# Order of the large and small matmuls in the column slots of a TensorE-bound block stack

## Chip, core and metric

The kernel runs on one core of one Trainium2 chip. The metric is the device time of one execution in microseconds (us); the kernel before takes 1665.5 us, the median of three runs.

## What is computed

Three transformer-like blocks over 256 tokens of width 1024, in float32: two layers of a first block and one of a second. Each has two gated feed-forward parts (FFN, inner width 2816) around a mixer. What matters here is the FFN and the second mixer, named sc:

```python
def swiglu(h, w_gate, w_up, w_down):
    return (jax.nn.silu(h @ w_gate) * (h @ w_up)) @ w_down
...
            p = h @ c_w_in[o]                       # 1024 -> 3 * 1024
            gate_b = p[..., :SC_WIDTH]
            gate_c = p[..., SC_WIDTH:2 * SC_WIDTH]
            xt = p[..., 2 * SC_WIDTH:]
            mix = (gate_b * causal_depthwise_conv(gate_c * xt, c_conv_w[o])) @ c_w_out[o]
```

## The kernel before

TensorE works on numbers split in two: a rounded high part in the type fp32r, and the low rest. A product of x and w is built as w_hi*x_hi + w_hi*x_lo + w_lo*x_hi, all added up in a PSUM bank.

The weights come from HBM as 564 slots of 128 x 1024 numbers into a ring `raw` of four. For each slot ACT writes the rounded part `w_hi` (line 1135), DVE the rest `w_lo` (line 1764 or 1768), both into a ring of eight, and PE uses it; the semaphore `lo_ready` tells PE that a slot is there, `slot_used` gives it back. SP issues the loads of `raw` in order (line 410). The order of work on each engine is written out by hand.

The eleven sub-stages run one after the other: ffn_0, ab, ffn_1, ctx_ffn, ffn_2, ctx_mix, sc, ffn_3, ffn_4, ssd, ffn_5. An FFN has eleven steps of 256 inner columns. In ffn_0 and in the first two and the last step of every FFN, gate and up products are made with tokens as the stationary operand (`wide_slot`, line 494). In the steps j = 2 to 9 of the other six FFN passes, and in all 24 input slots of sc, the weights are stationary: `column_slot` (lines 515 to 529). One such slot has the weights of 128 output columns for all eight k-tiles of the width of 1024 and fills one PSUM bank of 512 numbers for each partition. For each k-tile it issues two matmuls:

- a large one, with the 128 x 128 piece of `w_hi` stationary and 512 moving columns, the 256 tokens of the high part of hT and the 256 of its low part (`hT[:, :, k, :]`, two pieces of 256);
- a small one, with the piece of `w_lo` stationary and the 256 tokens of the high part alone, added onto the first half of the bank.

Each matmul has a weight load of its own. Even k-tiles issue large, small (lines 524 and 525) and odd ones small, large (lines 527 and 528), so that in a slot the order is L S S L L S S L and so on, and the last matmul, a large one, signals `slot_used`. The two halves of the bank are added up afterwards by ACT and DVE.

An FFN step with column slots (line 679 on) runs four of them, two for the gate in the banks `gu` and two for the up product in the banks `tp`, then the two down slots of the step before (`down`, line 539), each with 12 large matmuls whose moving operand is one piece of 512. A few transposes stand in between in the first steps. In sc, 24 column slots follow each other with other work between some. `col_slot` (line 509) is another helper, with small matmuls alone, used by other stages.

Of the kernel before, what the change touches and what calls it, by code (L numbers as in the profile page):

```python
# [23 lines left out]
KT = D // P  # L24
TOK = 256
TT = TOK // P
# [111 lines left out]
def build(nc, weights, ada_w, x_in, ctx_in, pre_rows, post_rows, small, mod, out):  # L138
    with ExitStack() as stack:
        def sb(name, shape, dt=F32):  # L140
            return stack.enter_context(nc.sbuf_tensor(name, shape, dt))

        def sem(name):
            return stack.enter_context(nc.semaphore(name))

        raw = sb("raw", [P, RAW, SLOT])
        w_hi = sb("w_hi", [P, RING, SLOT], F32R)
        w_lo = sb("w_lo", [P, RING, SLOT], F32R)
        hT = sb("hT", [P, 2, KT, TOK], F32R)
        hT_hi, hT_lo = hT[:, 0, :, :], hT[:, 1, :, :]  # L150
# [130 lines left out]
        hT_psum, hT_hi_ready, hT_lo_ready = sem("hT_psum"), sem("hT_hi_ready"), sem("hT_lo_ready")  # L281
# [47 lines left out]
        def any_bank(b):  # L329
            return dn_bank(b) if b < 4 else gu[:, b - 4, :] if b < 6 else tp[:, b - 6, :]  # L330
# [24 lines left out]
        def sc_bank(q):  # L355
            return any_bank(SC_BANKS[q])
# [32 lines left out]
        def column_bank(si):  # L389

            return (gu, tp)[si // 2][:, si % 2, :]
# [60 lines left out]
        def _(pe):  # L452
# [27 lines left out]
            def wide_slot(n, si, banks, used=True, between=lambda: None):  # L480

                if n < 2:
                    pe.wait_ge(lo_half, n + 1)
                else:
                    pe.wait_ge(lo_ready, n + 1)
                r = n % RING
                for kk in range(2):
                    if n < 2 and kk:
                        between()
                        pe.wait_ge(lo_ready, n + 1)  # L490
                    k = 2 * si + kk
                    for t, bank in banks.items():
                        for q, (h, w) in enumerate(((hT_hi, w_hi), (hT_lo, w_hi), (hT_hi, w_lo))):
                            m = pe.matmul(bank, h[:, k, t * P:(t + 1) * P],  # L494
                                          w[:, r, kk * 512:(kk + 1) * 512],
                                          start=k == 0 and q == 0, stop=k == KT - 1 and q == 2)
                if used:
                    m.then_inc(slot_used, 1)
                return m
# [12 lines left out]
                        m.then_inc(half_done, 1)  # L512
                m.then_inc(slot_used, 1)

            def column_slot(n, o, at_half=lambda: None):

                pe.wait_ge(lo_ready, n + 1)
                r = n % RING
                for k in range(KT):
                    if k == KT // 2:  # L520
                        at_half()
                    c = slice(k * P, (k + 1) * P)
                    if k % 2 == 0:
                        pe.matmul(o, w_hi[:, r, c], hT[:, :, k, :], start=k == 0, stop=False)  # L524
                        pe.matmul(o[:, 0:TOK], w_lo[:, r, c], hT_hi[:, k, :], start=False, stop=False)  # L525
                    else:
                        pe.matmul(o[:, 0:TOK], w_lo[:, r, c], hT_hi[:, k, :], start=False, stop=False)  # L527
                        m = pe.matmul(o, w_hi[:, r, c], hT[:, :, k, :], start=False, stop=k == KT - 1)  # L528
                m.then_inc(slot_used, 1)

            def down_slot(n, acts, k, start=False, stop=False, used=True):
# [95 lines left out]
            def ffn(s, n0):  # L627
# [3 lines left out]
                def act_transposed(j):  # L631
                    pe.wait_ge(act_ready, GATE_N[s, j, 1])
                    for t in range(TT):
                        for kk in range(2):
                            m = pe.transpose(tp[:, 0, kk * TOK + t * P:kk * TOK + (t + 1) * P],
                                             act_tok[:, t, kk * P:(kk + 1) * P], ident[:])
                    m.then_inc(actT_psum, 1)
# [8 lines left out]
                def down(n, j):  # L646
                    pe.wait_ge(actT_lo_ready, TURN_N[s, j, 1 if s and j == 0 else None])
                    for kk in range(2):
                        down_slot(n + kk, tokens_of(actT_hi, actT_lo, range(TT)), kk, start=j == 0 and kk == 0)
# [6 lines left out]
                def mod_transposed(group):  # L656
                    pe.wait_ge(ada_used, ADA_GROUP * (group + 1))
                    cols = mod_cols[:, ADA_GROUP * group:ADA_GROUP * (group + 1), :].rearrange("p i v -> p (i v)")
                    pe.transpose(tp[0:2 * ADA_GROUP, 1, 0:P], cols, ident[:]).then_inc(mod_turned, 1)
# [18 lines left out]
                for j in range(2, STEPS - 1):  # L678
                    n = n0 + 10 + 6 * (j - 2)
                    if s == 0:  # L680
                        if j > 2:
                            act_transposed(j - 1)
                        for si in range(4):
                            wide_slot(n + si, si, both)
                        down(n + 4, j - 1)
                        continue
                    for si in range(4):
                        if j > 2 and si % 2 == 0:
                            pe.wait_ge((gate_summed, up_summed)[si // 2], COLUMN_N[s, j - 1])
                        elif si == 2:  # L690
                            pe.wait_ge(actT_lo_ready, TURN_N[s, 1, None])
                        if si == 3 and (s, j - 1) in ADA_TURN:
                            pe.wait_ge(mod_biased, 1 + ADA_TURN[s, j - 1])
                        column_slot(n + si, column_bank(si))
                    down(n + 4, j - 1)
                    if (s, j) in ADA_TURN:
                        pe.wait_ge(up_summed, COLUMN_N[s, j])
                        mod_transposed(ADA_TURN[s, j])
# [23 lines left out]
                else:  # L722
                    for t in range(TT):
                        for si in range(4):
                            m = wide_slot(end + si, si, {t: gu[:, t, :]}, used=t == 1)
# [132 lines left out]
            def sc(s, n0):  # L858
                for q in range(3 * KT):
                    if q == 1:  # L860
                        context_x_tokens(1)
                    if q == 4:
                        context_b_tokens()
                    if q == 7:
                        context_states()
                    if q == 8:
                        pe.wait_ge(state_ready, 2)
                    if SC_BEFORE[q] is not None:
                        pe.wait_ge(sc_summed, SC_BEFORE[q] + 1)
                    if q:  # L870
                        column_slot(n0 + q, sc_bank(q))
                    else:
                        pe.wait_ge(hT_lo_ready, 2 * TT * s + TT)
                        column_slot(n0, sc_bank(0), lambda: pe.wait_ge(hT_lo_ready, 2 * TT * (s + 1)))
                out_proj(s, n0 + 3 * KT, range(KT), [[MIX0["sc"] + 1 + k // 2] * TT for k in range(KT)], apart=(0, 1))

            def dt_slot(n):
# [50 lines left out]
            def context_x_tokens(t):  # L928
                pe.wait_ge(conv_done, 4 + t)
                pe.wait_ge(xbc_ready, 3)  # L930
                for i in range(SSD_W // P):
                    m = turned_tile(x_cols[:, t * SSD_W + i * P:t * SSD_W + (i + 1) * P], 0, XS_T + i, t)
                if t:
                    m.then_inc(tokT_psum, 1)

            def context_b_tokens():
                pe.wait_ge(xbc_ready, 5)
                pe.wait_ge(p_ready, 1)
                for t, bank in enumerate((x_cols[:, TT * SSD_W:], x_cols[:, 0:512])):
                    if t:  # L940
                        pe.wait_ge(tok_ready, TT)
                    for i in range(SSD_G):
                        m = turned_tile(bank[:, i * P:(i + 1) * P], 0, BM_T + i, t)
                m.then_inc(tokT_psum, 1)

            def context_states():
                pe.wait_ge(tok_ready, 2 * TT)
                pe.wait_ge(xdt_ready, 2)
                for d in range(2):
                    for g in range(SSD_G):  # L950
                        for t in range(TT):
                            m = pe.matmul(dn[:, d, g * 256:g * 256 + GW], bm_tok[:, t, g * P:(g + 1) * P],
                                          x_dt_ctx[d][:, t, g * GW:(g + 1) * GW], start=t == 0, stop=t == 1)
                    m.then_inc(state_psum, 1)
# [173 lines left out]
            for s, name in enumerate(SUB):  # L1128
                {"ctx_mix": ctx_mix, "ab": ab, "sc": sc, "ssd": ssd}.get(name, ffn)(s, BASE[name])
# [1584 lines left out]
```

## Time and profile before

| what | value |
|---|---|
| median of three runs | 1665.5 us (1664.55 to 1665.92) |
| profiled execution | 1664.43 us |
| its span, first to last instruction | 1662.6 us |
| granted TensorE clock, mean | 0.999 |
| PE busy | 1654.5 us |
| PE weight loads busy | 1414.6 us |
| DVE busy | 1228.0 us |
| ACT busy | 928.0 us |
| large matmuls of column slots | 1728 |
| small matmuls of column slots | 1728 |

Matmuls are pipelined: a record's length reaches beyond the start of the next one, so what one costs on PE is the distance between starts. In the chain of waits a row covers these distances, not lengths. A timeline row shows the start and the length; rows of the same form that overlap can be merged, with their count.

### The profile page before, as it was taken

Reading aid. Unit: us, or ns where it says so; the run is one execution under the profiler, and the core shown is the slowest. Engines: PE = TensorE matmul, PEld = TensorE weight load, DVE = VectorE, ACT = ScalarE, POOL = GpSimd, SP = SyncE. Lnnn points to the kernel's source line nnn. Section 1 sums busy time; section 2 is a strip of 40 time slices with the busy share of each in tenths; the row PEclk is TensorE's granted clock in tenths of the full one; section 3 lists DMA queues with packets and bytes.
Section 4 is the critical chain, followed back from the end, with each engine's and each line's share of the span. In section 5 each row is a group of like instructions: output and inputs, shape, how many; then the busy total and the mean of one; then the engine's idle time right before and its main releaser. Section 6 shows DMA issues by size and latency. Waiting matters only on the chain.

```text
span 1662.6 us, 22804 instructions
## 1 busy us (share of the span) xinstructions
PE 1654.5 (100%) x8756; PEld 1414.6 (85%) x8756; DVE 1228.0 (74%) x1630; ACT 928.0 (56%) x1396; POOL 152.1 (9%) x210
## 2 busy tenths in 40 slices
PE   9999999999999999999999999999999999999998
PEld 7888888888888888888899888888888889988887
DVE  6888776788889777776688876655766568986564
ACT  6555577645555555555566455554645458655553
POOL 1100100000211001020010011000012011311000
PEclk9999999999999999999999999999999999999999
DMA  8977553787859776787655558654667546357551
GB/s 297 332 266 258 172 190 103 245 295 259 287 172 331 267 247 215 255 302 256 205 166 185 169 173 266 201 191 139 226 215 251 187 144 202 110 180 243 189 190 64
DMA packets 99356, 359.32 MB, mean 216 GB/s; under 512 B 11184, under 2 KB 11440, under 8 KB 99248
## 3 DMA queue, kind: packets, MB, share of 16 engines
q1 hardware_dynamic: 92736, 335.59, 59.6%
q0 software_dynamic: 6368, 22.21, 4.5%
q8 instruction: 69, 1.13, 0.3%
q14 instruction: 39, 0.32, 0.1%
q10 hardware_dynamic: 144, 0.07, 0.0%
HBM read 356.70 MB, written 1.12 MB: 215 GB/s over the span
## 4 chain that ended last, share of the span: by engine, by line
PE 98%; DVE 1%; DMA 0%; issue 0%; SPq 0%; ACT 0%; DVEq 0%; POOLq 0%; POOL 0%; ACTq 0%
PE dn L539 29%; PE gu L494 21%; PE gu L528 6%; PE tp L528 6%; PE gu L524 6%; PE tp L524 6%; PE dn L509 5%; PE gu L527 3%; PE tp L527 3%; PE gu L525 3%; PE tp L525 3%; PE tp L457 1%; PE gu L509 1%; PE dn L494 1%; PE dn L528 0%; PE dn L524 0%
## 5 line engine op out<-in xcount | busy, mean ns | idle before, releaser
L1768 DVE TENSOR_TENSOR w_lo<-raw,w_hi 128x1024 fp32r<-128x1024 f32 x520 | 639.5, 1240 | 216.3 <-ACT w_hi L1135 211.2
L1135 ACT ACTIVATE w_hi<-raw 128x1024 fp32r<-128x1024 f32 x520 | 549.5, 1059 | 319.5 <-PE dn L539 145.4
L494 PE MATMUL gu<-w_hi,hT 128*128 128x512 f32 x1056 | 328.9, 393 | 0.9 <-DVE w_lo L1764 0.5
L539 PE MATMUL dn<-w_hi,actT_hi 128*128 128x512 f32 x608 | 238.8, 393 | 0.0
L539 PE MATMUL dn<-w_lo,actT_hi 128*128 128x512 f32 x608 | 236.9, 390 | 0.0
L539 PE MATMUL dn<-w_hi,actT_lo 128*128 128x512 f32 x608 | 236.8, 389 | 0.0
L494 PEld LDWEIGHTS gu<-w_hi,hT 128*128 128x128 f32 x1056 | 195.6, 188 | 42.5 <-DVE hT L1776 1.4
L494 PE MATMUL gu<-w_lo,hT 128*128 128x512 f32 x528 | 205.8, 390 | 0.0
L524 PE MATMUL gu<-hT,w_hi 128*128 128x512 f32 x416 | 165.2, 397 | 0.0
L528 PE MATMUL gu<-hT,w_hi 128*128 128x512 f32 x416 | 164.6, 396 | 0.0
L524 PE MATMUL tp<-hT,w_hi 128*128 128x512 f32 x416 | 164.5, 396 | 0.0
L528 PE MATMUL tp<-hT,w_hi 128*128 128x512 f32 x416 | 164.5, 396 | 0.0
L1912 DVE CUSTOM_DVE_ANT_0 arena<-arena 128x1024 f32<-128x1024 f32 x112 | 135.0, 1231 | 0.3
L539 PEld LDWEIGHTS dn<-w_lo,actT_hi 128*128 128x128 f32 x608 | 114.1, 188 | 24.1
L539 PEld LDWEIGHTS dn<-w_hi,actT_lo 128*128 128x128 f32 x608 | 114.2, 188 | 23.4
L539 PEld LDWEIGHTS dn<-w_hi,actT_hi 128*128 128x128 f32 x608 | 114.2, 188 | 21.2
L494 PEld LDWEIGHTS gu<-w_lo,hT 128*128 128x128 f32 x528 | 99.1, 188 | 21.0
L527 PE MATMUL gu<-hT,w_lo 128*128 128x256 f32 x416 | 115.8, 278 | 0.0
L527 PE MATMUL tp<-hT,w_lo 128*128 128x256 f32 x416 | 115.8, 278 | 0.0
L525 PE MATMUL gu<-hT,w_lo 128*128 128x256 f32 x416 | 115.4, 277 | 0.0
L525 PE MATMUL tp<-hT,w_lo 128*128 128x256 f32 x416 | 115.4, 277 | 0.0
L2467 POOL TENSOR_SCALAR ms<-ssq 128x1 f32<-128x1 f32 x42 | 17.8, 425 | 926.4 <-ACT junk L1166 912.8
(366 smaller groups left out, 2506.2 us busy)
## 6 DMA issues: line engine op xcount, KB each, us to landing
raw<-in_weights SPq DMA_DIRECT2D x563, 512.0 KB, 4.3
arena<-in_ada_w SPq DMA_DIRECT2D x72, 512.0 KB, 4.4
post_row<-in_post_rows POOLq DMA_DIRECT2D x10, 512.0 KB, 6.2
pre_row<-in_pre_rows POOLq DMA_DIRECT2D x10, 512.0 KB, 7.4
mod_row<-mod POOLq DMA_DIRECT2D x9, 512.0 KB, 9.8
shift_row<-mod POOLq DMA_DIRECT2D x5, 512.0 KB, 10.0
x<-in_x_in SPq DMA_DIRECT2D x4, 256.0 KB, 5.7
arena<-in_c_rows POOLq DMA_DIRECT2D x2, 512.0 KB, 8.8
```

Source lines behind the costliest of these rows:

```text
L457: m = pe.transpose(in_bank(s, t, half)[:, q * P:(q + 1) * P], rows[:, t, k * P:(k + 1) * P], ident[:])
L494: m = pe.matmul(bank, h[:, k, t * P:(t + 1) * P], w[:, r, kk * 512:(kk + 1) * 512], start=k == 0 and q == 0, stop=k == KT - 1 and q == 2)
L509: m = pe.matmul(o, w[:, r, k * P:(k + 1) * P], h[:, k, :], start=k == 0 and q == 0, stop=k == KT - 1 and q == 2)
L524: pe.matmul(o, w_hi[:, r, c], hT[:, :, k, :], start=k == 0, stop=False)
L525: pe.matmul(o[:, 0:TOK], w_lo[:, r, c], hT_hi[:, k, :], start=False, stop=False)
L527: pe.matmul(o[:, 0:TOK], w_lo[:, r, c], hT_hi[:, k, :], start=False, stop=False)
L528: m = pe.matmul(o, w_hi[:, r, c], hT[:, :, k, :], start=False, stop=k == KT - 1)
L539: m = pe.matmul(dn[:, t, c], a[:, k, :], w[:, r, c], start=start and q == 0, stop=stop and q == 2)
L1135: act.activation(o, i, ACT.Copy, **kw).then_inc(done, 1)
L1768: dve.tensor_tensor(w_lo[:, r, :], raw[:, n % RAW, :], w_hi[:, r, :].bitcast(F32), ALU.subtract).then_inc(lo_ready, 1)
L1912: m = dve.tensor_tensor_reduce(ada_out[:, v, :], w, c_row[:, v, :], 1.0, 0.0, ALU.mult, ALU.add, mod_cols[:, i, v:v + 1])
L2467: pool.tensor_scalar(ms[:, c], ssq[:, c, 0], eps, None, ALU.add).then_inc(pool_step, 1)
```

## The change

`column_slot` gets a flag `lead`. Without it every k-tile issues large, small. With it k-tile 1 alone issues small, large, so that the slot begins L S S L and goes on L S L S. The flag is set in the first of the four slots of an FFN step and in the first slot of sc. The last matmul of a slot is now always a small one, and that one signals `slot_used`.

```diff
-            def column_slot(n, o, at_half=lambda: None):
+            def column_slot(n, o, at_half=lambda: None, lead=False):
 
                 pe.wait_ge(lo_ready, n + 1)
                 r = n % RING
@@ -520,12 +520,12 @@
                     if k == KT // 2:
                         at_half()
                     c = slice(k * P, (k + 1) * P)
-                    if k % 2 == 0:
+                    if lead and k == 1:
+                        pe.matmul(o[:, 0:TOK], w_lo[:, r, c], hT_hi[:, k, :], start=False, stop=False)
+                        pe.matmul(o, w_hi[:, r, c], hT[:, :, k, :], start=False, stop=False)
+                    else:
                         pe.matmul(o, w_hi[:, r, c], hT[:, :, k, :], start=k == 0, stop=False)
-                        pe.matmul(o[:, 0:TOK], w_lo[:, r, c], hT_hi[:, k, :], start=False, stop=False)
-                    else:
-                        pe.matmul(o[:, 0:TOK], w_lo[:, r, c], hT_hi[:, k, :], start=False, stop=False)
-                        m = pe.matmul(o, w_hi[:, r, c], hT[:, :, k, :], start=False, stop=k == KT - 1)
+                        m = pe.matmul(o[:, 0:TOK], w_lo[:, r, c], hT_hi[:, k, :], start=False, stop=k == KT - 1)
                 m.then_inc(slot_used, 1)
...
-                        column_slot(n + si, column_bank(si))
+                        column_slot(n + si, column_bank(si), lead=si == 0)
...
-                        column_slot(n0, sc_bank(0), lambda: pe.wait_ge(hT_lo_ready, 2 * TT * (s + 1)))
+                        column_slot(n0, sc_bank(0), lambda: pe.wait_ge(hT_lo_ready, 2 * TT * (s + 1)), lead=True)
```

## Rows read from the trace of the kernel before

**Rows 1.** The page: busy time of the engines, granted clock by slice, chain by engine.
```profile
PE 1654.5 (100%) x8756; PEld 1414.6 (85%) x8756; DVE 1228.0 (74%) x1630; ACT 928.0 (56%) x1396; POOL 152.1 (9%) x210
...
PEclk9999999999999999999999999999999999999999
...
PE 98%; DVE 1%; DMA 0%; issue 0%; SPq 0%; ACT 0%; DVEq 0%; POOLq 0%; POOL 0%; ACTq 0%
```

**Rows 2.** Waits of PE: us in total, times, longest us.
```profile
PE dn L594 <- DVE actT_hi L2441: 1.5, 1, 1.5
PE gu L494 <- DVE w_lo L1764: 0.5, 1, 0.5
PE gu L494 <- DVE w_lo L1768: 0.3, 1, 0.3
```

**Rows 3.** Timeline of PE, a step's column slots: start us, length us, line, tiles.
```profile
558.48 0.39 PE L539 MATMUL dn<-w_lo,actT_hi 128*128 128x512 f32 x1
558.71 0.39 PE L524 MATMUL gu<-hT,w_hi 128*128 128x512 f32 x1
...
559.16 0.40 PE L528 MATMUL gu<-hT,w_hi 128*128 128x512 f32 x1
559.40 0.40 PE L524 MATMUL gu<-hT,w_hi 128*128 128x512 f32 x1
...
561.49 0.39 PE L524 MATMUL gu<-hT,w_hi 128*128 128x512 f32 x1
561.72 0.28 PE L525 MATMUL gu<-hT,w_lo 128*128 128x256 f32 x1
561.83 0.28 PE L527 MATMUL gu<-hT,w_lo 128*128 128x256 f32 x1
561.95 0.40 PE L528 MATMUL gu<-hT,w_hi 128*128 128x512 f32 x1
562.18 0.40 PE L524 MATMUL gu<-hT,w_hi 128*128 128x512 f32 x1
562.42 0.28 PE L525 MATMUL gu<-hT,w_lo 128*128 128x256 f32 x1
562.53 0.27 PE L527 MATMUL gu<-hT,w_lo 128*128 128x256 f32 x1
562.65 0.40 PE L528 MATMUL gu<-hT,w_hi 128*128 128x512 f32 x1
```

**Rows 4.** Timeline of PE: end of these slots, first and 23rd matmul of down.
```profile
569.62 0.40 PE L528 MATMUL tp<-hT,w_hi 128*128 128x512 f32 x1
569.85 0.39 PE L539 MATMUL dn<-w_hi,actT_hi 128*128 128x512 f32 x1
...
574.84 0.39 PE L539 MATMUL dn<-w_hi,actT_lo 128*128 128x512 f32 x1
```

**Rows 5.** Chain that ended last, in order of time: start us, us, count.
```profile
865.79 11.52 PE dn L509 x96
```

**Rows 6.** By line, lengths min/median/max ns: steady stretches, then line 525 throughout.
```profile
L524 PE MATMUL gu<-hT,w_hi x7: 393/397/398, 559.4 to 563.6; 128*128 128x512 f32 x7
L525 PE MATMUL gu<-hT,w_lo x7: 277/277/278, 559.6 to 563.8; 128*128 128x256 f32 x7
L527 PE MATMUL gu<-hT,w_lo x8: 274/278/283, 559.0 to 563.9; 128*128 128x256 f32 x8
L528 PE MATMUL gu<-hT,w_hi x8: 395/396/396, 559.2 to 564.0; 128*128 128x512 f32 x8
L539 PE MATMUL dn<-w_hi,actT_lo x8: 389/389/389, 570.1 to 574.8; 128*128 128x512 f32 x8
L509 PE MATMUL dn<-hT,w_hi x64: 283/283/283, 865.6 to 876.9; 128*128 128x256 f32 x64
L525 PE MATMUL gu<-hT,w_lo x416: 276/277/282, 324.0 to 1623.1; 128*128 128x256 f32 x139
```

**Rows 7.** Groups by line of the whole span: count, busy us, mean ns, idle before.
```profile
L524 PE MATMUL gu<-hT,w_hi 128*128 128x512 f32 x416 | 165.2, 397 | 0.0
L524 PE MATMUL tp<-hT,w_hi 128*128 128x512 f32 x416 | 164.5, 396 | 0.0
L524 PE MATMUL dn<-hT,w_hi 128*128 128x512 f32 x32 | 12.6, 395 | 0.0
```

**Rows 8.** Waits of all engines: us in total, times, longest us.
```profile
ACT w_hi L1135 <- PE dn L539: 154.3, 114, 1.7
ACT silu L1135 <- PE gu L528: 77.1, 50, 1.7
ACT w_hi L1135 <- PE gu L494: 51.5, 53, 1.7
ACT w_hi L1135 <- PE gu L528: 49.8, 43, 2.0
```

## The prediction

> **What bounds the kernel now.** I read the engines' shares first. TensorE (PE) is busy for 1654.5 of 1662.6 us, at a granted clock of nine tenths or more in every slice of the span, and 98% of the chain that ended last is PE's [rows 1]. Its sequencer waited 2.3 us in all, three times, the longest 1.5 us [rows 2]. So the time is the sum of the distances from one matmul's start to the next, and the reader has to look at starts: the recorded busy lengths overlap. The 64 matmuls of a step's four column slots run from 558.71 to 569.85 us [rows 3, 4]. That is 11.14 us, or sixteen pairs of k-tiles of four matmuls each: large, small, small, large ("L S S L"), where L has 512 columns and S has 256.
>
> I then ask what each size costs alone. Twenty-two L of line 539 in a row lie between 569.85 and 574.84 us [rows 4]: 4.99 / 22 = 0.2268 us each. Ninety-six S of line 509 take 11.52 us [rows 5]: 0.1200 us each. Two of each would be 0.6936 us. The sixteen pairs are not equal: the first, behind down-slot matmuls, runs from 558.71 to 559.40, 0.69 us, and the other fifteen from 559.40 to 569.85 [rows 3, 4], 10.45 / 15 = 0.6967 us each. So an L S S L pair among its like costs 3.1 ns more than its parts do in streams of their own. That excess is what an order can win back in the ordinary way.
>
> Where it sits can be read from recorded lengths. In the clean streams the length stands over the distance to the next start by a fixed amount: L 389 ns against 226.8 (162 more), S 283 ns against 120.0 (163 more) [rows 4 to 6]. Taking that amount off [rows 6]: L behind S (line 528) is 396 long, so about 234 ns; L behind L (line 524) lies between 393 and 398, 231 to 236 ns; S behind L (line 525) is 277, 114 ns; S behind S (line 527) swings from 274 to 283, 111 to 120 ns. The timeline shows the swing as alternate pairs: 0.39 and 0.40 us for L524, 0.28 and 0.27 for L527 [rows 3]. An S directly behind an L starts its successor early (114, not 120), and the next L pays it back (234, not 227). What isn't explained by that give and take is the second L, which could take 227 and takes 231 to 236.
>
> **The change, part by part.** 1. What moves. Column slots fill 864 pairs of k-tiles (2 x 416 for the banks gu and tp, and 32 for dn, of line 524) [rows 7]. From now on every odd k-tile is L S too. The flag `lead` keeps the old order in the first pair of the first slot of each step: eight steps in each of six FFN passes is 48, and one slot of stage sc, 49 in all. 864 - 49 = 815 pairs turn from L S S L into L S L S. No matmul, weight load, DMA, wait or byte is added or removed; SP's, POOL's, ACT's and DVE's queues hold the same instructions in the same order.
>
> 2. The price of a changed pair. In L S L S every L stands behind an S and every S behind an L; only lengths of lines 528 and 525 stand for those places. Carried over as they are: 2 x (234 + 114) = 696, or with the ends of rounding 695 to 696. Against 696.7 that is about 1.3 ns less. The other reading is that the excess belongs to the second L behind an S pair, which no longer occurs; then the pair costs its parts, 693.6, which is 3.1 ns less. Over 815 pairs: -1.1 us to -2.5 us. I take -2.0 us, nearer the second, because the 234 of line 528 is met in full by give-back (227 + 6) and holds no loss, while the 0.69 us of the first pair of a step, whose first L stands behind an L of an undisturbed stream, shows that the L S S L group itself can run at its parts' price [rows 3].
>
> 3. The bounds of that price. The L places have shown 393 to 398 and the S places 274 to 278 outside S behind S [rows 6]. Lowest: 2 x (231 + 111) = 684 in length arithmetic, but S behind L has never been under 276 over the whole span [rows 6], so 2 x (231 + 113) = 688, -8.7 ns a pair, -7.1 us. Highest among ordinary lengths: 2 x (236 + 115) = 702, +5.3 ns, +4.3 us.
>
> 4. The ends of slots. A slot now ends with an S. Its last result is there at start + length. Before, this was 396 - 234 = 162 ns after the next slot's first start; now it is 277 - 114 = 163 ns. Nothing moves for the evacuations of ACT or for the release of the ring slot. Cost 0. Cover for the weight side: ACT's `w_hi` waits 154.3 + 51.5 + 49.8 us for PE to release slots, and `silu` 77.1 us for PE to finish [rows 8], so both are ahead of PE and stay so after a gain of some 0.05 us a step. If the cover were gone, PE would wait for `w_lo`; the longest such wait now is 0.5 us [rows 2]. The at-half wait of the first sc slot stays at k-tile 4. The 49 kept pairs and the joint from each to the next k-tile (one L behind L as before) cost what they cost now: 0.
>
> Sum: profiled execution 1664.4 us (span 1662.6 and 1.8 around it) - 2.0 = 1662.4 us. The median of the runs shown is 1.1 us above the profiled one, so the forecast is 1665.5 - 2.0 = 1663.5 us.
>
> What a measurement of this kernel can tell from no change is about 0.2%, 3.3 us, or 4.1 ns a changed pair. My forecast lies inside that.
>
> **The rivals.** A. The slow place locks in (slower). Now L behind L alternates between 393 and 397 or 398, and the slow one is followed by S at its ordinary 277 [rows 3, 6]. If an L that is directly followed by an S settles on the slow value each time, because no second S is there to swing back to 274, the pair is 2 x (236 + 115) = 702: +4.3 us, 1669.8 us. It is slower than before from an L S couple of 348.3 ns upwards. For it: the slow value is seen only in an L that an S follows. Against it: line 528's L, behind an S, never swings (395 to 396).
>
> B. The fast place locks in (faster). The same alternation settles on 231 and 113: -7.1 us, and with S at its usual 114, 690 ns and -5.5 us; together about 1659 us. For it: half of the pairs already show 231. Against: those are behind an L; the L behind an S pays back.
>
> C. Order does not matter. The excess could belong to the L itself, since it streams two pieces of 256 (high and low part of hT) and the 227 ns streams read one piece. Then the pair stays 696.7 and the time 1665.5 us. The first pair, with the same two pieces at 0.69 us, speaks against it weakly (the timeline is rounded to 10 ns).
>
> The Trainium skill speaks for C. In "TensorE: Matmul & The Clock Gate", section "Back-to-back issue gap", the start-to-start distance is the columns over 2.4 GHz plus 2.5 ns, whatever stood before. By it a pair would cost 650 ns in either order and the change nothing. The rows give 697, with neighbours' influence in every small one, so the trace doesn't bear the rule out to the nanosecond. The same page, section "LDWEIGHTS (loading the stationary operand)", gives 107 ns for a load of 128 columns, about as long as an S streams. With one load under each matmul in either order, that too makes no difference of the order.
>
> **How the numbers follow.** Forecast (mixed places, -1.1 to -2.5 us, with a spread that reaches below -3.3) 0.45; B 0.22; C 0.13; A 0.17; something larger of either sign, a place not seen in this trace, 0.03. The range reaches to B's low end, 1665.5 - 7.1 = 1658.4, and a little below, for a small matmul that no second one follows has no row: 1657.5. Above it takes in A: 1669.8. Faster by over 0.2%: B and a quarter of the forecast, 0.33. Slower by over 0.2%: A and a share of the unseen, 0.18. Within: 0.49.
>
> **What would show it.** In the changed kernel's timeline a step's 64 column matmuls should take 0.69 + 15 x 0.694 = 11.10 us instead of 11.14 (B: 11.01, C: 11.14, A: 11.22). Large lengths should stand at one value near 396 and small ones near 277, with no 283 but in the first pair of a step. PE's waits should stay at 2 to 3 us. The forecast is wrong if a length outside 393 to 398 or 274 to 283 shows up in steady state, or if PE begins to wait for `w_lo` or for a bank: then the cover of point 4 wasn't there.

## The result, and the profile after

The changed kernel takes 1673.84 us (median of six runs, 1672.32 to 1674.87) against 1664.86 us for the kernel before beside it: 9.0 us or 0.52% longer, ratio 1.0052 with a 95% interval of 1.0042 to 1.0062. I had forecast 1663.5 us and a range up to 1669.8. It is slower, and by more than any of my cases gave.

The page of the changed kernel, its span, busy times and the chain by engine:

```profile
span 1672.8 us, 22804 instructions
PE 1663.4 (99%) x8756; PEld 1418.2 (85%) x8756; DVE 1229.9 (74%) x1630; ACT 928.4 (56%) x1396; POOL 150.6 (9%) x210
...
PE 95%; DVE 2%; DMA 2%; issue 0%; ACT 0%; POOL 0%; SPq 0%; DVEq 0%; POOLq 0%; ACTq 0%
```

The span grew by 10.2 us and PE's busy time by 8.9; the busy times of DVE, ACT and POOL are those of [rows 1] within 2 us, and the chain is still PE's, to 95%. PE's waits (us in total, times, longest us):

```profile
PE dn L594 <- DVE actT_hi L2441: 1.5, 1, 1.5
PE gu L494 <- DVE w_lo L1768: 0.7, 2, 0.4
PE gu L494 <- DVE w_lo L1764: 0.5, 1, 0.5
PE tp L457 <- DMA x<-in_x_in: 0.3, 1, 0.3
PE tp L457 <- DVE xn L1813: 0.2, 1, 0.2
PE gu L527 <- DVE hT L1776: 0.2, 1, 0.2
```

They are 3.4 us against 2.3 in [rows 2]; those on `w_lo` are 1.2 us against 0.8. PE did not run out of work; it took longer for the same work. The timeline of one FFN step behind a down slot, from the last matmul of down to the first of the next down, and then the first matmul of the next step:

```profile
560.94 0.39 PE L539 MATMUL dn<-w_lo,actT_hi 128*128 128x512 f32 x1
561.17 0.39 PE L527 MATMUL gu<-hT,w_hi 128*128 128x512 f32 x1
561.39 0.28 PE L528 MATMUL gu<-hT,w_lo 128*128 128x256 f32 x1
561.51 0.28 PE L524 MATMUL gu<-hT,w_lo 128*128 128x256 f32 x1
561.62 0.40 PE L525 MATMUL gu<-hT,w_hi 128*128 128x512 f32 x1
561.86 0.40 PE L527 MATMUL gu<-hT,w_hi 128*128 128x512 f32 x1
...
572.44 0.40 PE L539 MATMUL dn<-w_hi,actT_hi 128*128 128x512 f32 x1
...
577.95 0.39 PE L527 MATMUL gu<-hT,w_hi 128*128 128x512 f32 x1
```

The column slots take 572.44 - 561.17 = 11.27 us (11.28 by the trace's nanoseconds) against 11.14 in [rows 3, 4]; the kept pair at the head takes 0.69 us as before. The 24 down matmuls behind them, which nobody touched, take 577.95 - 572.44 = 5.51 us; before, they took 5.44. The recorded lengths (min/median/max ns) of this step, of a step in ffn_4 and of the sc stage:

```profile
L527 PE MATMUL tp<-hT,w_hi x16: 395/398/403, 566.8 to 572.1; 128*128 128x512 f32 x16
L528 PE MATMUL tp<-hT,w_lo x16: 277/281/284, 567.0 to 572.3; 128*128 128x256 f32 x16
...
L527 PE MATMUL tp<-hT,w_hi x16: 391/391/391, 1209.9 to 1215.1; 128*128 128x512 f32 x16
L528 PE MATMUL tp<-hT,w_lo x15: 280/280/280, 1210.1 to 1215.0; 128*128 128x256 f32 x15
...
L527 PE MATMUL dn<-hT,w_hi x51: 392/395/395, 924.9 to 953.4; 128*128 128x512 f32 x51
L528 PE MATMUL dn<-hT,w_lo x52: 274/277/280, 924.8 to 953.6; 128*128 128x256 f32 x52
```

These are the key rows. In the stretches shown the order is large, small in all three places, yet there are three patterns. Large matmuls reach 403 ns, a length that [rows 6] doesn't have, in the first; in the second all are 391, in the third 392 to 395. Read as distances between starts in the trace's nanoseconds (large, small, large, small, ...):

- 47 of 48 FFN steps: 233, 117, 241, 120, 236, 113 and over again, 1060 ns for three k-tiles, 353.3 for one. I call it the slow cycle.
- one step of ffn_4 (at 1205 us): 230, 117 and over again, 346.7 for one.
- the long run in sc: 231, 113, 232, 118 in some order, 346.7 for one as well. These two are fast cycles. The old order had 348.3 for a k-tile.

Sc has two shorter runs too, of 24 k-tiles each, which start behind transposes. Both come before the long one, and one was fast and the other slow (lengths of large matmuls):

```profile
L527 PE MATMUL tp<-hT,w_hi x16: 391/391/391, 897.6 to 902.8; 128*128 128x512 f32 x16
...
L527 PE MATMUL gu<-hT,w_hi x15: 395/398/403, 904.3 to 909.3; 128*128 128x512 f32 x15
```

So the slow cycle is not a thing of the FFN alone.

The accounts: 40 steps take 0.135 us more in the column slots and 0.059 more in down, 7.8 us; seven steps behind transposes take 0.145 more and 0.012 less, 0.9 us; the step of ffn_4 and sc give back 0.2. That is 8.5 us of the 10.2 in the span. The other 1.7 us lie outside these stretches, in stalls that come and go between executions: PE's time outside the column slots and the down slots behind an FFN step's is 790.8 us in the trace before, 792.4 in this one and between 790.3 and 792.3 in those of the experiments.

### The profile page after: what moved, and what is told of

Read it like the earlier page. It is cut to its first block, busy times and chain, and to the rows that moved or that the text cites. A ratio compares the mean times of both kernels' runs of the same rounds, so it can differ in the third digit from the quotient of the medians.

```text
span 1672.8 us, 22804 instructions
## 1 busy us (share of the span) xinstructions
PE 1663.4 (99%) x8756; PEld 1418.2 (85%) x8756; DVE 1229.9 (74%) x1630; ACT 928.4 (56%) x1396; POOL 150.6 (9%) x210
## 4 chain that ended last, share of the span: by engine, by line
PE 95%; DVE 2%; DMA 2%; issue 0%; ACT 0%; POOL 0%; SPq 0%; DVEq 0%; POOLq 0%; ACTq 0%
PE dn L539 29%; PE gu L494 20%; PE tp L527 12%; PE gu L527 11%; PE tp L528 6%; PE gu L528 6%; PE dn L509 3%; DMA raw<-in_weights 1%; PE dn L527 1%; DVE w_lo L1768 1%; PE tp L457 1%; PE dn L494 1%; PE gu L525 1%; PE dn L528 0%; PE tp L635 0%
## 5 line engine op out<-in xcount | busy, mean ns | idle before, releaser
L527 PE MATMUL tp<-hT,w_hi 128*128 128x512 f32 x832 | 295.9, 398 | 0.0
L527 PE MATMUL gu<-hT,w_hi 128*128 128x512 f32 x783 | 281.0, 398 | 0.2 <-DVE hT L1776 0.2
L528 PE MATMUL gu<-hT,w_lo 128*128 128x256 f32 x783 | 219.5, 280 | 0.0
L527 PEld LDWEIGHTS tp<-hT,w_hi 128*128 128x128 f32 x832 | 156.3, 188 | 38.6
L527 PEld LDWEIGHTS gu<-hT,w_hi 128*128 128x128 f32 x783 | 147.3, 188 | 33.7 <-DVE hT L1776 0.5
L528 PEld LDWEIGHTS tp<-hT,w_lo 128*128 128x128 f32 x832 | 157.1, 189 | 0.0
L528 PEld LDWEIGHTS gu<-hT,w_lo 128*128 128x128 f32 x783 | 147.9, 189 | 3.6
```

Source lines behind the costliest of these rows:

```text
L528: m = pe.matmul(o[:, 0:TOK], w_lo[:, r, c], hT_hi[:, k, :], start=False, stop=k == KT - 1)
```

## Experiments

Two theories were set against each other. T1: the order large, small has several steady cycles of different cost, and what stands before the run picks the one it falls into. T2: this order costs 353.3 ns a k-tile in the FFN by itself. In the diffs, which are cut to the lines that matter and stand against the kernel before, L is the large and S the small matmul; `order` is the list in which a slot issues them.

**Strict order, no kept pair.**

```diff
+                order = [(big, k) for k in range(KT) for big in ((False, True) if k in swapped else (True, False))]     # swapped=() in every slot
```

> Every k-tile of every column slot issues large, small; the kept pair (small, large at k-tile 1 of a step's first slot) is gone. In the changed kernel the steady gaps repeated over three k-tiles as 233, 117, 241, 120, 236, 113 ns (353.3 ns a k-tile) in 46 or so of 48 FFN steps, but 230, 117 (346.7 ns a k-tile) in one step and 231, 113, 232, 118 in the long sc run. Theory T1 (the entry picks a cycle out of several that the order L S allows): with another entry all steps that follow a down slot fall into one cycle, which may be the fast one: 32 k-tiles at 346.7 ns make a step's slots 11.09 us and the kernel 1662 to 1663 us; if it is the slow one again 11.3 us and 1674 us, but then the first few gaps must differ from the changed kernel's and the cycle be reached in another way. Rival T2 (the order L S L S costs 353.3 ns a k-tile in the FFN by itself, whatever stands before): 11.3 us a step, 1674 us, the same three-tile cycle. Fast here decides for T1.

Measured: 1674.27 us, ratio 1.0055 (1.0039 to 1.0072). Behind a down slot all steps take 11.290 us and go into the slow cycle at once: 227, 113, 233, 117, 241, 120, 236, 113. The lengths are those of the changed kernel:

```profile
L526 PE MATMUL tp<-hT,w_hi x16: 395/398/403, 567.0 to 572.3; 128*128 128x512 f32 x16
L528 PE MATMUL tp<-hT,w_lo x15: 277/281/284, 567.2 to 572.2; 128*128 128x256 f32 x15
```

Two steps whose run starts directly behind a single transpose took 11.178 us, in the cycle 230, 117, where in the changed kernel the same two were slow. So the kept pair is not what makes the change slow, and the same place can be in either cycle. The time alone fitted both theories; the two steps spoke for T1.

**Only sc changed.**

```diff
+                        column_slot(n + si, column_bank(si), swapped=range(1, KT, 2))      # FFN: the old order
...
+                        column_slot(n0, sc_bank(0), lambda: pe.wait_ge(hT_lo_ready, 2 * TT * (s + 1)), swapped=(1,))      # sc: as changed
```

> FFN steps keep the order of the kernel before, the 24 sc slots have that of the changed kernel. If the parts add up as in the two traces (the sc slots were 0.15 us shorter in all, the FFN steps with the down slots behind them some 8.7 us longer), this kernel is 0.1 to 0.3 us faster than before: no difference to be measured, FFN steps 11.14 us each with four matmuls in 696.4 ns, the long sc run 47.3 us against 47.5. If instead the sc slots hand a slower cycle on to what follows them, ffn_3 and later steps are longer than before.

Measured: 1664.53 us beside 1664.96, ratio 0.9997 (0.9988 to 1.0007). The long sc run took 47.28 us against 47.52, in a fast cycle: 3.5 ns less a pair, a little more than the 1.3 to 3.1 that I had forecast for the whole change, but it holds for a small part. FFN steps kept 11.14 us. The two shorter runs of sc, whose instructions are those of the changed kernel, changed places: here the first was slow and the second fast.

```profile
L526 PE MATMUL tp<-hT,w_hi x16: 395/398/403, 893.1 to 898.4; 128*128 128x512 f32 x16
...
L526 PE MATMUL gu<-hT,w_hi x15: 391/391/396, 900.0 to 904.8; 128*128 128x512 f32 x15
```

So behind transposes the order of the instructions alone does not fix the cycle: the same ones, in a kernel that differs only elsewhere, went the other way.

**First slot old, the other three new.**

```diff
+                        column_slot(n + si, column_bank(si), swapped=range(1, KT, 2) if si == 0 else ())
```

> The first slot of each FFN step has the whole old order (L S S L four times), the other three are strictly large, small. T1 (entry picks the cycle): the last old pair hands over at another phase than the first one did, at a gap of 231 or 236 where the kept pair left at 236; the three strict slots then run at 346.7 or 353.3 ns a k-tile, so a step's slots take 2.78 + 8.31 = 11.10 us or 2.78 + 8.48 = 11.27 us; nothing between. T2 (the order alone): 11.27 us, 1665 + 48 x 0.13 + 2.4 for down = 1673.5 us.

Measured: 1671.15 us, ratio 1.0039 (1.0026 to 1.0052). Steps behind down take 11.257 us: 2.782 for the old slot, then 231 for the first new large matmul and 113, 233, 117, 241, 120, 236 over and again. Down behind it took 5.449 us, hardly more than before's 5.444, though the cycle was the slow one. The step is left at another place of the cycle (the first large matmul of down is at 236 here, at 241 in the changed kernel), and what down has to pay differs with it.

**All large first.**

```diff
+                order = [(big, k) for big in (True, False) for k in range(KT)]
```

> Each column slot issues its eight large matmuls first and then its eight small ones: one change of size in each direction for a slot instead of four (before) or eight (changed). If a change of size is what costs, the slot comes near its parts, 8 x 226.7 + 8 x 120.0 = 2773.6 ns against 2785.6 before and 2819 changed: a step 11.10 us, the kernel 2.6 us faster than before. If only the cycle matters in which alternating sizes lock, this order has none to lock into in its plain stretches and costs the same 2774 to 2780 ns: no difference between these two here, but it prices the change of size: over 2790 ns a slot would say that small matmuls in a row, not the alternation, are dear.

Measured: 1667.20 us, ratio 1.0014 (1.0004 to 1.0023). The first large matmul of each of the four slots of a step, and the first of down:

```profile
559.54 0.39 PE L526 MATMUL gu<-hT,w_hi 128*128 128x512 f32 x1
...
562.30 0.40 PE L526 MATMUL gu<-hT,w_hi 128*128 128x512 f32 x1
...
565.10 0.40 PE L526 MATMUL tp<-hT,w_hi 128*128 128x512 f32 x1
...
567.89 0.40 PE L526 MATMUL tp<-hT,w_hi 128*128 128x512 f32 x1
...
570.68 0.40 PE L539 MATMUL dn<-w_hi,actT_hi 128*128 128x512 f32 x1
```

By the trace's nanoseconds the first slot, behind large matmuls, takes 2766 ns and the other three 2793 each, 20 more than the parts and over the 2790 of my expectation; down takes 5.467 us. The distances show why: of eight small ones in a row the last six run at 120, and then the five large ones behind them take 233, 236, 228, 233, 231 instead of 226.7. So one passage from large to small and back costs 20 ns net after a long run of small ones, against 3.1 ns in L S S L. By the mark that I had set, small matmuls in a row are dear, and not the alternation alone.

**Seven entries in one kernel.**

```diff
+ENTRY = {3: "LSSL" + "LS" * 6, 4: "LLSS" + "LS" * 6, 5: "LSLLSS" + "LS" * 5, 6: "L" + "LS" * 7 + "S",
+         7: "LLLSSS" + "LS" * 5, 8: "LLLLSSSS" + "LS" * 4, 9: "LSLSSL" + "LS" * 5}
...
+                        column_slot(n + si, column_bank(si), order=ENTRY.get(j, "LS" * KT) if si == 0 else "LS" * KT)
```

> Slots 2 to 4 of every step are strictly large, small; the first slot differs by step, six steps of each kind: j=3 L S S L then L S; j=4 L L S S then L S; j=5 L S L L S S then L S; j=6 L then L S seven times then S; j=7 L L L S S S then L S; j=8 L L L L S S S S then L S; j=9 L S L S S L then L S. T1 (several cycles, the entry picks one): the seven kinds split into two sorts, steps whose last three slots take 24 x 346.7 = 8320 ns and steps where they take 24 x 353.3 = 8480 ns, the same sort for all six steps of a kind that stand behind a down slot. At least one of the six new entries is fast. T2 (after steady large matmuls this order always costs 353.3): all take 8480 ns.

One execution, 1670.32 us. Measured, from the starts in the trace; the column slots of all steps of a kind that stand behind down (five or six each) agree within 2 ns:

| step | first slot | slots 2 to 4, ns | slots, us | down behind, us |
|---|---|---|---|---|
| 3 | L S S L, L S ... | 8480 | 11.277 | 5.503 |
| 4 | L L S S, L S ... | 8480 | 11.286 | 5.467 |
| 5 | L S L L S S, L S ... | 8320 | 11.093 | 5.467 |
| 6 | L, L S ..., S | 8481 | 11.286 | 5.467 |
| 7 | L L L S S S, L S ... | 8480 | 11.284 | 5.449 |
| 8 | L L L L S S S S, L S ... | 8480 | 11.270 | 5.503 |
| 9 | L S L S S L, L S ... | 8320 | 11.112 | 5.481 |

The lengths in the second half of steps 4 and 5, one after the other in the same pass, and the ends of step 5's column slots:

```profile
L530 PE MATMUL tp<-hT,w_hi x16: 395/398/403, 549.2 to 554.5; 128*128 128x512 f32 x16
L530 PE MATMUL tp<-hT,w_hi x16: 392/394/395, 565.8 to 571.0; 128*128 128x512 f32 x16
...
560.30 0.39 PE L530 MATMUL gu<-hT,w_hi 128*128 128x512 f32 x1
...
571.39 0.39 PE L543 MATMUL dn<-w_hi,actT_hi 128*128 128x512 f32 x1
```

That settles T1 against T2. Slots 2 to 4 are the same instructions in steps 4 and 5; only six matmuls at the head of the step, of the same kinds and number, stand in another order, and a cycle of 346.7 instead of 353.3 ns a k-tile holds for all three slots behind them. For runs that start behind down, then, the order at the head decides. It is not so behind a transpose: the entry of step 9, fast in its five steps behind down, was slow in the one step where a transpose stood at the head (8480 ns for slots 2 to 4).

**The old order from the same entries.**

```diff
+ENTRY = {3: "LSLS" + "LSSL" * 3, 4: "LLSS" + "LSSL" * 3, 5: "LSLLSSLS" + "LSSL" * 2, 6: "L" + "LSSL" * 3 + "LSS",
+         7: "LLLSSSLS" + "LSSL" * 2, 8: "LLLLSSSS" + "LSSL" * 2, 9: "LSLSSLLS" + "LSSL" * 2}
...
+                        column_slot(n + si, column_bank(si), order=ENTRY.get(j, "LSSL" * (KT // 2)) if si == 0 else "LSSL" * (KT // 2))
```

> Slots 2 to 4 of every step have the old order L S S L; the first slot differs by step: j=3 L S L S first, j=4 L L S S, j=5 L S L L S S L S, j=6 the old order one place later (L, then L S S L), j=7 L L L S S S L S, j=8 L L L L S S S S, j=9 L S L S S L L S, each then on with L S S L. If the old order too has several cycles of which the entry picks one (T1 in its general form), slots 2 to 4 take 8357 ns in some kinds and another value (8320 if there is a cycle without excess, more if there is a slow one) in others. If small matmuls in pairs bring the old order back to the same cycle from every entry, all kinds show 8357 ns within 5 ns: then the old order is robust where the new one is not.

One execution, 1667.60 us. Slots 2 to 4 took 8355 to 8360 ns from the entries of steps 3, 4, 5, 7, 8 and 9; from that of step 6, whose first slot ends L S S, the second slot took 12 ns more once, 8373. The steady lengths are those of [rows 6] whatever the entry, here in steps 4 and 6:

```profile
L530 PE MATMUL tp<-hT,w_hi x16: 393/396/398, 549.6 to 555.0; 128*128 128x512 f32 x16
L530 PE MATMUL tp<-hT,w_hi x15: 393/396/398, 582.8 to 587.7; 128*128 128x512 f32 x15
```

So L S S L falls back into one cycle of 696.7 ns from each of eight entries (these seven and its own). This is what the trace of before could not show: its steadiness was a property of that order. That the pair of small ones does it is argued, not shown.

**What a cycle depends on: pieces, sizes, loads.** One feature of the large or small matmul was changed in each FFN pass but ffn_1, so this kernel and the next leave out parts of the product; only distances are read from them, from one execution each (1682.07 and 1679.43 us). All column slots have the order L S.

```diff
+VARIANT = {"ffn_1": None, "ctx_ffn": "one piece", "ffn_2": "small of 384", "ffn_3": "short load of large",
+           "ffn_4": "short load of small", "ffn_5": "second half"}      # short load: 64 weight columns
```

> Strictly large, small everywhere; in each FFN pass one feature of the first seven k-tiles of a slot is another, so that parts of the product are wrong or left out. ffn_1: none (353.3 ns a k-tile, of which 6.7 over the parts). ctx_ffn: the large one streams one piece of 512 numbers (two k-tiles of the high part) instead of two pieces: if the jump between pieces costs, the k-tile falls to 346.7; if not, 353.3. ffn_2: the small one streams 384 columns, parts 226.7 + 173.3 = 400.0 ns: if the excess comes from a weight load (about as long as 256 columns stream) that does not quite fit under a small matmul, the k-tile takes 400; if it comes from a change of size as such, about 406. ffn_3: the large one's weights are 64 columns, so that the load under the small one is half as long: load theory 346.7 or less, otherwise 353.3. ffn_4: the small one's weights are 64 columns, the load under the large one: both theories 353.3. ffn_5: the small one adds onto the second half of the bank instead of the first: 353.3 unless the order of PSUM writes matters.

The groups of lengths, in the order one piece, 64 columns for L, S of 384, S onto the second half:

```profile
L528 PE MATMUL tp<-hT,w_hi x112: 391/398/403, 515.8 to 638.1; 128*128 128x512 f32 x112
L530 PE MATMUL tp<-hT,w_hi x96: 389/389/395, 1034.1 to 1154.1; 128*64 128x512 f32 x96
L535 PE MATMUL tp<-hT,w_lo x112: 338/338/338, 703.2 to 837.6; 128*128 128x384 f32 x112
L539 PE MATMUL tp<-hT,w_lo x112: 277/281/284, 1523.7 to 1646.2; 128*128 128x256 f32 x112
```

ffn_1, unchanged, took 11.290 us behind down as in the strict order. One piece: 403 is still there and the steps behind down took 11.290 us, so the jump between the pieces is innocent. Second half of the bank: the same 11.290. A large matmul with 64 weight columns: lengths of 389, those of the clean stream, and 226.7 + 113.3 = 340.0 ns a k-tile, without excess over the parts; my expectation was 346.7 or less. Small matmuls with 64 weight columns (ffn_4): 346.6 ns a k-tile and 11.117 us a step, where both theories had 353.3; nothing here explains that miss. So the small one's weight columns count as well, be it in the cost or in the pick of the cycle. Small matmuls of 384 columns: 237.5 + 176 = 413.4 ns in the last two slots of a step, where I expected 400 if a load that does not quite fit under 256 columns were the whole story. Half as many columns again leave the excess in place, so that form of the load theory falls. Timeline of this variant, one k-tile in 0.41 us:

```profile
706.23 0.39 PE L532 MATMUL tp<-hT,w_hi 128*128 128x512 f32 x1
706.46 0.34 PE L535 MATMUL tp<-hT,w_lo 128*128 128x384 f32 x1
706.64 0.40 PE L532 MATMUL tp<-hT,w_hi 128*128 128x512 f32 x1
```

With 384 columns, too, there are two values. In the first slot of each step behind down the same instructions take 406.8 ns a k-tile (231 to 233 and 175), and only later 413.4; the large lengths of the first and the third slot of one step:

```profile
L532 PE MATMUL gu<-hT,w_hi x7: 393/393/395, 733.7 to 736.2; 128*128 128x512 f32 x7
...
L532 PE MATMUL tp<-hT,w_hi x6: 398/398/398, 740.2 to 742.2; 128*128 128x512 f32 x6
```

**More sizes.**

```diff
+VARIANT = {"ffn_1": (64, 64, TOK), "ctx_ffn": (96, P, TOK), "ffn_2": (32, P, TOK), "ffn_3": (P, P, 320),
+           "ffn_4": (P, P, 128), "ffn_5": (64, P, 384)}      # weight columns of L, of S; moving columns of S
```

> Strictly large, small; in k-tiles 1 to 6 of a slot sizes are changed, so parts of the product are left out. Theory L (load law, from the 64-column run and the plain streams): a matmul takes its columns over 2.4 GHz plus 13.3 ns for the load of 128 weight columns under it, in proportion to the load, and the excess over that sum comes only with a full load under a small matmul. ffn_1 (64 weight columns for both): 220.0 + 113.3 = 333.3 ns. ctx_ffn (96 for the large): 226.7 + 116.7 = 343.3. ffn_2 (32 for the large): 226.7 + 110.0 = 336.7. ffn_3 (small one streams 320): 226.7 + 146.7 = 373.3, and if it behaves like the one of 384 (414 against 400) some 10 more. ffn_4 (small one streams 128): limited by the load, 226.7 + 109 = 336, or more. ffn_5 (small of 384, 64 weight columns for the large): 226.7 + 166.7 = 393.3. Rival M (a fixed 13.3 ns for each matmul, the 340 of the 64-column run being a cycle by chance): 346.7 or 353.3 in the first three, 374 to 387 in the fourth, 400 or more in the last.

Measured distances for a k-tile, from the starts in the trace:

| L weights, S weights, S columns | measured, ns | theory L |
|---|---|---|
| 64, 64, 256 | 227 + 113 = 340 | 333.3 |
| 96, 128, 256 | 347 (224 + 120 and 232 + 118 in turn) | 343.3 |
| 32, 128, 256 | 227 + 113 = 340 | 336.7 |
| 128, 128, 320 | 233 + 147 = 380 in the first slot, 378 in the others | 373.3 (+ 10) |
| 128, 128, 128 | 280 + 60 = 340 | 336 |
| 64, 128, 384 | 232.5 + 174.5 = 407 | 393.3 |

The small matmuls of the last row and of the first, as groups (count, busy us, mean ns, idle); less the 162 ns by which their lengths stand over the distances they are 174 and 112 ns:

```profile
L527 PE MATMUL tp<-hT,w_lo 128*128 128x384 f32 x96 | 32.2, 336 | 0.0
...
L527 PE MATMUL tp<-hT,w_lo 128*64 128x256 f32 x96 | 26.3, 274 | 0.0
```

Theory L falls as a law: the measured values lie 3 to 14 ns over its sums. With 64 weight columns for the large matmul, 64 or 128 for the small one make no difference, 340 both times, and neither do 32 against 64 for the large one. The fixed cost of rival M falls too, for 340 is under its 346.7. What both size runs leave standing is narrow: with 256 moving columns for the small matmul and 64 or 32 weight columns for the large one, neither cycle appears, 340.0 ns against 346.7 or 353.3. With 384 moving columns the 64-column load does not remove the excess: 406.8 ns is also what the full load shows in the first slot of a step, so there the short load at most keeps the stream out of the slower value. And a large matmul with 64 weight columns not only has a shorter load under the small one before it, it also fills half as many partitions of its bank; the two were not told apart.

**The fast entry used.**

```diff
+FAST_IN = "LSLLSS" + "LS" * 5
+OLD_OUT = "LS" * 6 + "LSSL"
...
+                        column_slot(n + si, column_bank(si), order={0: FAST_IN, 3: OLD_OUT}.get(si, "LS" * KT))
```

> The order of the changed kernel with another entry and another end: the first slot of a step is L S L L S S and then L S five times, slots 2 and 3 are L S, slot 4 is L S six times and then L S S L. In the run with seven entries this entry led to 346.7 ns a k-tile in all six steps behind a down slot (11.093 us a step). T1 (the entry picks the cycle and the cycle is the whole cost of the change): all steps behind a down slot stay at 346.7 ns; a step's slots take 11.09 to 11.10 us and the down slots behind them 5.45 to 5.47 instead of 5.50; the kernel comes to 1663 to 1664.5 us, 1 to 2 us below the kernel before and 10 below the changed one. T2 (the extra time of the changed kernel has a further source in the order L S): 1670 us or more.

Measured: 1665.42 us beside 1665.06, ratio 0.9999 (0.9990 to 1.0008). That is 8 to 9 us below the changed kernel with the same matmuls in nearly the same order, as T1 says, but not the gain of 1 to 2 us. All 42 steps j=3 to 9 were fast, 11.095 us, or 11.195 where a transpose stands at their head; the six steps j=2 behind four transposes stayed in the slow cycle (11.376 us instead of 11.240, 0.8 us in all), and L S S L at the end made down longer, not shorter (5.478 against 5.467). I had not thought of the first and guessed wrong on the second.

```diff
+                        column_slot(n + si, column_bank(si), order=OLD if j == 2 else NEW if si else FAST_IN)
```

> Each step behind a down slot (42 of 48) has L S L L S S and then L S five times in its first slot and L S in the other three, to the end; the six steps j=2, behind transposes, where this entry led to 353.3 ns a k-tile, keep the old order; sc is strictly L S. T1: the 42 steps take 11.093 us and 5.467 us for the down slots behind them, 26 ns less than before's 11.142 + 5.444; 42 x 26 = 1.1 us, with 0.2 us from sc 1.3 us in all: 1663.6 us where before stands at 1664.9, which is within what can be told from no change. T2 (a second source of time in the new order): 1666 us or more. The steps of j=2 take 11.24 us as before in both.

Measured: 1663.87 us beside 1665.05, 1.2 us less, ratio 0.9993 (0.9984 to 1.0002). The interval holds 1, so it is not shown to beat the kernel before; the trace shows the parts: 11.093 us in 40 steps, 11.193 in the two behind a transpose, 11.240 in the six of j=2. A step of it:

```profile
559.33 0.39 PE L542 MATMUL dn<-w_lo,actT_hi 128*128 128x512 f32 x1
559.56 0.39 PE L529 MATMUL gu<-hT,w_hi 128*128 128x512 f32 x1
...
570.65 0.39 PE L542 MATMUL dn<-w_hi,actT_hi 128*128 128x512 f32 x1
...
576.12 0.39 PE L529 MATMUL gu<-hT,w_hi 128*128 128x512 f32 x1
```

570.65 - 559.56 = 11.09 us, and 5.47 for down: 16.56 us, where the changed kernel has 16.78 and the one before 16.59. The new order is not slow in itself; entered behind down as the change enters it, it is.

## Why the prediction was wrong

**The bound.** It held. PE's starts are the time; the other engines went on waiting for PE.

**Point 1, what moves,** held: 815 pairs, nothing else.

**Point 2, the price of a changed pair,** is the step that failed. I priced a large matmul by its neighbour on the left and put 234 + 114 together. That gives 695 to 696 a pair, and 693.6 for the parts. Something near the second does occur: in the long run of sc and in one FFN step a pair takes 693.3. But neighbours don't set these distances: the order of six matmuls at the head of a step changes all that follow in its column slots, which settle into a cycle. The alternate pairs of [rows 3, 6] were a sign: two pairs with the same neighbours and different lengths. I read them as a spread about a mean, where they are the stations of one cycle. All 40 steps behind down and seven of the eight behind transposes took 706.7, 10.0 ns more than before's pair, where I had put 2.5 less. The 0.69 us of the first pair, on which I leaned, was no sign of a cheap steady pair: in the changed kernel that pair still takes 0.69 us and the slow cycle follows it.

**Point 3, the bounds.** 702 was built from lengths that the old order shows (up to 398). The slow cycle has 403, a value of no ordinary matmul before. The term was mis-sized: bounds from rows of one order did not bound another.

**Point 4, the ends of slots,** held for evacuation and ring, as far as PE's waits show (3.4 us in all). It was silent about the stage behind: down's first ten large matmuls run at 224 to 241 ns after the slow cycle and cost 59 ns a step, 2.4 us over 40 steps. I had the price of what a run leaves behind at nothing without naming it. The down slots of before, at 5.444 us against 24 x 226.7 = 5.441, gave little hint; but behind the eight steps that start with transposes the same 24 matmuls took 5.461 us, so what ran before them already counted in that trace, and I had not looked.

**The rivals.** A (the slow place locks in) had the direction and the kind of mechanism, with 702 instead of 706.7 for a pair and no price for down: 4.3 us against 8.5. I gave it 0.17. B (688 to 690) occurred nowhere at these sizes: the fast cycle that sc and the entries of steps 5 and 9 found is 693.3, the low end of my forecast. In these cycles small ones of 112 to 118 stand with large ones of 230 to 233. C (no influence of order) is refuted by steps 4 and 5 of the run with seven entries; the two pieces, its reason, are refuted as well.

## What to carry to other kernels

Where one engine is full, the price of an order of long and short matmuls with full weight loads cannot be put together from the prices of neighbours. Measure the order with the entry that it will have, and read starts at full resolution for a repeating pattern. Several entries can be tried in one kernel, one for each step of a loop. Behind a steady stream one execution was enough here; behind a transpose it was not, for the same instructions went either way. And look at the stage behind a changed stretch: it can pay part of the bill.

## What the runs showed of the hardware

- The same instruction stream settles into one of at least two steady cycles on TensorE, 346.7 or 353.3 ns for a matmul of 512 and one of 256 columns with 128 weight columns each. Behind down slots the column slots of all steps of a kind agree within 2 ns, so there it is not noise. Behind transposes it varies: in the changed kernel five of six steps behind four transposes were slow, after 314 ns for the first large matmul, and the one of ffn_4 was fast, after 317. The 3 ns don't tell the two apart: both short runs of sc began with 314 there, and the first was fast and the second slow, while with the same instructions in the run where only sc was changed it was the other way round. What decides there is open.
- The order L S S L comes back to one cycle, 696.7 ns for the four, from eight entries.
- With 64 instead of 128 weight columns for the large matmul, loaded under a small one of 256 moving columns, both cycles are gone: 226.7 + 113.3 ns. The Trainium skill ("TensorE: Matmul & The Clock Gate", section "Back-to-back issue gap") gives columns over 2.4 GHz plus 2.5 ns for the isolated distance, and says that in a stream of loads and matmuls both set the spacing, which the prediction left out. Here the large ones never came under 224 ns, where an estimate by that formula is 215.8, and the small ones of 256 columns never under 112, where it is 109.2.
- The effect of small matmuls on large ones reaches over five of them after a run of eight, and over up to ten after the slow cycle; left at another place of that cycle, it reaches over one (236, then 226.7).

What in the array makes the cycles is open: no record shows when a matmul enters it apart from when it is started. That the weight columns of the large matmul belong to it is shown by the runs with 64 and 128 of them; whether by the load or by the size of the matmul itself is not, nor why with 384 moving columns 7 ns of excess stay even at 64.
